# Forgetting attention in a hybrid layer kernel: values with tokens on partitions, the reciprocal sum applied at evacuation, and three PSUM banks in rotation

## The chip, the cores and the metric

The kernel runs on one core of one Trainium2 chip. The metric is the device time of one execution in microseconds. All runs of the kernel before: 3224.91, 3225.07 and 3237.13 us, with the median at 3225.07 us.

## The reference, cut to what matters

The reference advances a two-layer model by one step, for a prompt of 512 tokens and a sample of 32 new tokens behind a cache of 512. Each layer has a mixer (three branches: forgetting attention, differential attention, an RWKV scan), cross attention and a SwiGLU block. The change touches only the forgetting attention ("FoX"), with 8 heads of 64:

```python
def block(qb, dqb, pb):
    s = jnp.einsum('bqhd,bkhd->bhqk', qb, k_all).astype(jnp.float32) * scale
    s = s + jnp.swapaxes(dqb, 1, 2)[:, :, :, None] - d_k[:, :, None, :]
    mask = kpos[None, None, None, :] <= pb[:, None, :, None]
    p = jax.nn.softmax(jnp.where(mask, s, -jnp.inf), axis=-1)
    return jnp.einsum('bhqk,bkhd->bqhd', p.astype(v_all.dtype), v_all)
```

Everything is float32. The output of this branch is later multiplied by a branch weight, with the 512 feature rows on partitions and the T = 544 tokens along the free dimension.

## The kernel before, in words

The kernel is written engine by engine: one instruction stream each for PE (TensorE), ACT (ScalarE), DVE (VectorE), POOL (GpSimd) and SP (DMA issue), each in the order in which its code issues it, tied together by counting semaphores. A loop runs over the two layers. In each layer the forgetting attention runs between the input projections and the differential attention, as four pairs of heads (`it`). Each pair has 10 tiles: for head h, four query tiles of 128 prompt tokens (i = 0..3, with (i+1)·128 keys) and one tile of the 32 sample tokens (i = 4, with 544 keys). `FOX_TILES` (line 104) gives their order.

The work on a pair is a software pipeline over steps k, with the same k in every engine's stream:

- PE, lines 833 to 880: `fox_prologue(h)` at k = 0 and k = 4 transposes values (job "v", line 800), new keys (job "k", line 805) and cached keys (job "p", line 809). At every k: `fox_scores(k)` (lines 823 and 828, with a bf16 mask matmul after it), then `late(s)` (line 774), then `fox_turn(k-2)`, which transposes the exponentials (line 840, or 844 for the sample tile), then `fox_values(k-3)` (line 858, or 862 and 864 for the sample tile). At k = 8, `late` comes ahead of the scores.
- `late(s)` is a quarter of a dense projection of other columns of the input weight: 12 matmuls of four 128-deep slices by three terms of a split float32 product. It accumulates in PSUM bank 7. A half is evacuated by ACT in `late_put` (line 1419) before the next half may begin, and the waits on it (`late_evac`) are in `late`.
- DVE: `fox_scale(h)` (line 1915) at k = 0 and 4; `fox_max(k)` (line 1903), a row maximum; `fox_norm(k-1)` (lines 1910 and 1912), which takes the reciprocal of the sum and multiplies the exponentials by it; `late_split` (line 1891) after k = 3, k = 8 and the last step, which splits the next weight unit of `late` into a high and a low part (lines 1809 and 1819, both of 128x1024); and `fox_evac(h)` (lines 1923 and 1924), once a head, ahead of `fox_max(8)` and at the end. In the first pair of a layer, three memsets of the second buffer (lines 1944 and 1945) stand after the `late_split` of k = 3.
- ACT: `fox_exp(k)` (line 1338) with the sum as accumulator, `late_put` at every second k (even in the first pair, odd in the others), `fox_put(k-2)`, which copies the transposed exponentials out of PSUM, and the copies of the prologue (all line 1341).
- POOL stores, SP loads; each waits on semaphores of the others.

PSUM has 8 banks. Scores use banks 0 to 2 (the sample tile bank 2 and 3), transposes use banks 4 and 5 in turn (`put_bank`), the values of a pair accumulate in bank 6 with head h on partitions 64h to 64h+63 (the sample tile in bank 3), bank 7 is `late`'s.

## Time and profile before

| | |
|---|---|
| median of three runs | 3225.07 us |
| the profiled execution | 3224.55 us |
| its span | 3223.0 us |
| PE busy | 2917.9 us (91%) |
| DVE busy | 1618.5 us (50%) |
| ACT busy | 721.0 us (22%) |
| mean granted clock of PE | 0.96 of full |

A matmul's row shows its latency, and successive matmuls overlap, so the pace of a group is read from the starts of successive rows or from the chain of waits. PE's weight loads have rows of their own (PEld). In forms such as `128*64 128x128`, the first part is the stationary operand (128 rows by 64 columns), the second the moving one. A float32 matmul of the program shows as two matmul rows and two load rows; a transpose shows as one.

### The profile page before, as it was taken

Reading aid. Unit: us, or ns where it says so; the run is one execution under the profiler, and the core shown is the slowest. Engines: PE = TensorE matmul, PEld = TensorE weight load, DVE = VectorE, ACT = ScalarE, POOL = GpSimd, SP = SyncE. Lnnn points to the kernel's source line nnn. Section 1 sums busy time; section 2 is a strip of 40 time slices with the busy share of each in tenths; the row PEclk is TensorE's granted clock in tenths of the full one; section 3 lists DMA queues with packets and bytes.
Section 4 is the critical chain, followed back from the end, with each engine's and each line's share of the span. In section 5 each row is a group of like instructions: output and inputs, shape, how many; then the busy total and the mean of one; then the engine's idle time right before and its main releaser. Section 6 shows DMA issues by size and latency. Waiting matters only on the chain.

```text
span 3223.0 us, 69431 instructions
## 1 busy us (share of the span) xinstructions
PE 2917.9 (91%) x26468; PEld 2692.0 (84%) x26468; DVE 1618.5 (50%) x2997; ACT 721.0 (22%) x1777; POOL 246.4 (8%) x425
## 2 busy tenths in 40 slices
PE   7999998899789889999989999889997898899998
PEld 6877777888788769999978777778897887799998
DVE  4444552666574245553364444426665742455533
ACT  1133332222212230000112333322222122200001
POOL 1121111000000100000001211110000000000000
PEclk9999998999899999999988999999998999899999
DMA  4443326222153213232224333262221521232222
GB/s 122 134 120 91 109 86 148 77 68 64 40 156 95 68 53 92 85 89 79 75 81 122 104 99 111 77 159 74 70 66 47 161 82 53 66 91 85 84 83 64
DMA packets 421640, 292.44 MB, mean 91 GB/s; under 512 B 38640, under 2 KB 386448, under 8 KB 421216
## 3 DMA queue, kind: packets, MB, share of 16 engines
q1 hardware_dynamic: 399072, 229.75, 25.7%
q0 software_dynamic: 22272, 58.70, 5.7%
q8 instruction: 190, 3.11, 0.4%
q14 instruction: 106, 0.87, 0.1%
HBM read 233.23 MB, written 55.18 MB: 89 GB/s over the span
## 4 chain that ended last, share of the span: by engine, by line
PE 74%; DVE 12%; DVEq 4%; issue 4%; ACT 3%; DMA 2%; POOLq 1%; ACTq 1%; SPq 0%; POOL 0%
PE PS L708 32%; PE PS L774 9%; PE PS L1079 7%; PE PS L1020 5%; PE PS L686 4%; DVE WLO L1819 2%; PE PS L1233 2%; ACT U L1338 2%; PE PS L945 1%; PE PS L1058 1%; PE PS L858 1%; PE PS L823 1%; DMA U<-in_rwkv_g_dram 1%; PE PS L1144 1%; ACT U L1341 1%
## 5 line engine op out<-in xcount | busy, mean ns | idle before, releaser
L708 PE MATMUL PS<-U_r,WHI 128*128 128x272 f32 x2656 | 485.3, 294 | 70.4 <-DVEq L1820 35.3
L1809 DVE CAST WHI<-ring 128x1024 fp32r<-128x1024 f32 (+2 forms) x292 | 189.5, 649 | 623.7 <-PE PS L708 472.1
L708 PEld LDWEIGHTS PS<-U_r,WHI 128*128 128x128 f32 x2656 | 395.6, 193 | 78.4 <-issue 50.8
L1341 ACT COPY U<-PS 128x272 f32<-128x272 f32 (+10 forms) x764 | 265.9, 373 | 807.1 <-PE PS L1079 144.9
L708 PE MATMUL PS<-brT_r,WHI 128*128 128x272 f32 x1728 | 360.3, 290 | 1.9 <-ACTq L1720 1.9
L708 PE MATMUL PS<-U_r,WLO 128*128 128x272 f32 x1696 | 356.7, 292 | 0.0
L708 PE MATMUL PS<-hT_r,WHI 128*128 128x272 f32 x1696 | 350.7, 288 | 0.0
L1819 DVE TENSOR_TENSOR WLO<-ring,WHI 128x1024 fp32r<-128x1024 f32 (+2 forms) x292 | 332.3, 1138 | 23.5 <-issue 1.8
L774 PE MATMUL PS<-U_r,WHI 128*128 128x272 f32 x832 | 268.6, 323 | 16.1 <-ACT U L1341 16.1
L708 PE MATMUL PS<-brT_r,WLO 128*128 128x272 f32 x1344 | 278.2, 288 | 0.0
L708 PEld LDWEIGHTS PS<-brT_r,WHI 128*128 128x128 f32 x1728 | 274.7, 190 | 2.3 <-ACTq L1720 2.3
L1020 PE MATMUL PS<-U_r,WHI 128*128 128x272 f32 x768 | 237.4, 309 | 42.2 <-POOLq L401 26.8
L708 PEld LDWEIGHTS PS<-U_r,WLO 128*128 128x128 f32 x1696 | 273.2, 193 | 0.0
L708 PEld LDWEIGHTS PS<-hT_r,WHI 128*128 128x128 f32 x1696 | 267.6, 189 | 0.0
L774 PE MATMUL PS<-U_r,WLO 128*128 128x272 f32 x832 | 247.3, 297 | 0.0
L774 PE MATMUL PS<-hT_r,WHI 128*128 128x272 f32 x832 | 246.5, 296 | 0.0
L1020 PE MATMUL PS<-U_r,WLO 128*128 128x272 f32 x768 | 227.1, 296 | 0.0
L1020 PE MATMUL PS<-hT_r,WHI 128*128 128x272 f32 x768 | 226.2, 295 | 0.0
L1079 PE MATMUL PS<-U 64*64 64x64 f32 (+1 forms) x5184 | 215.9, 238 | 2.4 <-issue 1.8
L1079 PEld LDWEIGHTS PS<-U 64*64 64x64 f32 x5184 | 208.5, 134 | 5.1 <-issue 3.9
L708 PEld LDWEIGHTS PS<-brT_r,WLO 128*128 128x128 f32 x1344 | 209.8, 189 | 0.0
L774 PEld LDWEIGHTS PS<-U_r,WHI 128*128 128x128 f32 x832 | 164.8, 198 | 36.3 <-ACT U L1341 21.9
(321 smaller groups left out, 4407.0 us busy)
## 6 DMA issues: line engine op xcount, KB each, us to landing
ring<-in_w_in_dram SPq DMA_DIRECT2D x126, 512.0 KB, 4.1
ring<-in_w_ffn_in_dram SPq DMA_DIRECT2D x88, 512.0 KB, 3.8
ring<-in_w_ffn_out_dram SPq DMA_DIRECT2D x32, 448.0 KB, 3.6
proj_scratch<-U POOLq DMA_DIRECT2D x104, 136.0 KB, 2.0
U<-proj_scratch SPq DMA_DIRECT2D x48, 272.0 KB, 4.1
gate_scratch<-U POOLq DMA_DIRECT2D x96, 136.0 KB, 3.0
U<-gate_scratch SPq DMA_DIRECT2D x48, 272.0 KB, 2.8
ring<-in_w_branch_dram SPq DMA_DIRECT2D x48, 256.0 KB, 3.0
```

What stands on the lines that cost most here:

```text
L686: ins = mm(PS[0:width, 2 * q + h, 0:HT], ring[:, n % RING, k, 0:width], rhs(k, h), start=(k == 0), stop=(k == kn - 1))
L708: ins = mm(PS[:, 2 * q + h, 0:HT], w, half(x, h), start=(first and k == 0 and n == 0), stop=(last and k == kn - 1 and n == len(terms) - 1))
L774: ins = mm(PS[:, 7, 0:HT], w, half(x, h), start=(k == 0 and i == 0), stop=(k == 7 and i == 2))
L823: mm(PS[:, b, 0:n], q, FK[it % 2][0:66, h, 0:n], start=True, stop=False)
L858: ins = mm(PS[o, 6, i * P:(i + 1) * P], FVT[it % 2][:, h, t, :], FPT[:, k % 2, t * P:(t + 1) * P], start=(t == 0), stop=(t == i))
L1020: ins = mm(PS[:, 6 + h, 0:HT], w, half(x, h), start=(k == 0 and i == 0), stop=(k == 7 and i == 2))
L1079: ins = mm(PS[r, bank, cols], w_c[r], x_c[r], start=(n == 0), stop=(n == len(pairs) - 1))
L1233: ins = mm(PS[:, 2 + n % 4, u * P:(u + 1) * P], MNT[:, k, t * P:(t + 1) * P], ring[:, (U_MEM + 2 * s + u) % RING, k, :], start=(k == 0), s ...
L1338: return act.activation(out, in_, func, **kw)
L1341: return act.copy(out, in_)
L1809: copy(hi, src)
L1819: tt(lo, w, hi.bitcast(F32), ALU.subtract)
```

## The change

- Values: the transposed exponentials become the stationary operand and the values the moving one, so that tokens stand on the partitions of the output (128 tokens by 64 columns) in place of features (64 partitions by 128 columns). Each of the 10 tiles of a pair has its own output, in its own turn of a PSUM bank.
- `fox_norm` goes. `fox_inverse` keeps only the reciprocal. `fox_evac(k)` multiplies by it as it copies the tile's 128x64 result from PSUM into `FO`, 10 times a pair, at DVE step k+4, in place of one copy of 64x512 and one of 64x32 a head.
- `fox_final(pair)` transposes `FO` (five transposes, two bank turns) and ACT copies the result to `brT`. It runs at k = 2 of the next pair, or ahead of the differential attention for the last pair.
- Banks 4, 5 and 6 rotate over all jobs of the layer (`FOX_ORDER`: prologue jobs, transposes t, values o, final jobs f). A job waits for the evacuation of the job three places earlier: by ACT (`fx_put`), or by DVE for an o (`fx_evac`).
- `fox_scores(8)` moves ahead of `late`; `fox_turn` waits for the exponential itself; the sample tile's scores no longer wait for an evacuation of bank 3.
- On DVE the third `late_split` moves from after the last `fox_norm` to step 12, between `fox_evac(8)` and `fox_evac(9)`.

```diff
+def fox_jobs():
+    order = []
+    for it in range(4):
+        for k in range(13):
+            if k in (0, 4):
+                order += [(it, x, k // 4) for x in "vkp"]
+            if k == 2 and it > 0:
+                order += [(it - 1, "f", n) for n in range(2)]
+            if 2 <= k <= 11:
+                order.append((it, "t", k - 2))
+            if k >= 3:
+                order.append((it, "o", k - 3))
+    order += [(3, "f", n) for n in range(2)]
+    return order
+FOX_ORDER = fox_jobs()
+FOX_BANK = {key: 4 + n % 3 for n, key in enumerate(FOX_ORDER)}
+FOX_LAST = {key: FOX_ORDER[n - 3] if n >= 3 else None for n, key in enumerate(FOX_ORDER)}
...
-                    def put_bank():
-                        j = job[0]
-                        job[0] += 1
-                        pe.wait_ge(fx_put, g * 16 + j + 1)
+                    def put_bank(key):
+                        last = FOX_LAST[key]
+                        if last is not None:
+                            if last[1] == "o":
+                                pe.wait_ge(fx_evac, l * FOX_OUTS + FOX_COUNT[last])
+                            else:
+                                pe.wait_ge(fx_put, l * FOX_PUTS + FOX_COUNT[last])
                         settle(pe)
-                        return PS[:, 4 + j % 2, :]
+                        return PS[:, FOX_BANK[key], :]
...
                     def fox_values(k):
                         h, i = FOX_TILES[k]
-                        pe.wait_ge(fx_put, g * 16 + jobs_of[k] + 1 + 2)
-                        if i == 0:
-                            pe.wait_ge(fx_evac, g * 2 + h + 1)
-                        o = slice(64 * h, 64 * h + 64)
+                        pe.wait_ge(fx_put, l * FOX_PUTS + FOX_COUNT[(it, "t", k)])
+                        settle(pe)
+                        b = put_bank((it, "o", k))
                         if i < 4:
                             for t in range(i + 1):
-                                ins = mm(PS[o, 6, i * P:(i + 1) * P], FVT[it % 2][:, h, t, :],
-                                         FPT[:, k % 2, t * P:(t + 1) * P], start=(t == 0), stop=(t == i))
+                                ins = mm(b[:, 0:64], FPT[:, k % 2, t * P:(t + 1) * P], FVT[it % 2][:, h, t, :],
+                                         start=(t == 0), stop=(t == i))
...
+                    def fox_final(pair):
+                        pe.wait_ge(fx_evac, l * FOX_OUTS + 10 * (pair + 1))
+                        settle(pe)
+                        b = put_bank((pair, "f", 0))
+                        for i in range(4):
+                            ins = tr(b[:, i * P:(i + 1) * P], FO[:, i, :], ident)
+                        ins.then_inc(fx_turned, 1)
+                        b = put_bank((pair, "f", 1))
+                        tr(b[:, 0:DEC_SEQ], FO[0:DEC_SEQ, 4, :], ident[0:DEC_SEQ, 0:DEC_SEQ]).then_inc(fx_turned, 1)
...
-                        if k < 10 and k != 8:
+                        if k < 10:
                             fox_scores(k)
                         if k < (12 if it else 11):
                             late(12 * it + k + (0 if it else 1))
-                        if k == 8:
-                            fox_scores(k)
+                        if k == 2 and it > 0:
+                            fox_final(it - 1)
...
-                        ts(FP[0:m, k % 3, 0:n], FP[0:m, k % 3, 0:n], FST[0:m, k % 3, 2:3], None, ALU.mult) \
-                            .then_inc(fx_norm, 1)
...
+                    def fox_evac(k):
+                        h, i = FOX_TILES[k]
+                        m = P if i < 4 else DEC_SEQ
+                        dve.wait_ge(fx_out, g * 10 + k + 1)
+                        ts(FO[0:m, i, 64 * h:64 * h + 64], PS[0:m, FOX_BANK[(it, "o", k)], 0:64], FST[0:m, k % 4, 2:3], None,
+                           ALU.mult).then_inc(fx_evac, 1)
+                    for k in range(14):
                         if k == 0:
                             fox_scale(0)
                         if k == 4:
                             fox_scale(1)
-                        if k == 8:
-                            fox_evac(0)
+                        if k >= 4:
+                            fox_evac(k - 4)
                         if k < 10:
                             fox_max(k)
-                        if k >= 1:
-                            fox_norm(k - 1)
+                        if 1 <= k <= 10:
+                            fox_inverse(k - 1)
+                        if k == 12:
+                            late_split(3 * it + 2)
                         if k in (3, 8):
                             late_split(3 * it + k // 8)
...
-                    late_split(3 * it + 2)
-                    fox_evac(1)
```

## Rows read from the trace of the kernel before

**Rows 1.** The page's chain of work that ended last, shares of the span.
```profile
PE 74%; DVE 12%; DVEq 4%; issue 4%; ACT 3%; DMA 2%; POOLq 1%; ACTq 1%; SPq 0%; POOL 0%
```
**Rows 2.** Windows of the four pairs, layers 0 and 1: start:end, length, busy per engine, clock.
```profile
131.70:305.40 173.70, 163.38 (x1159) 132.31 (x1159) 74.97 (x167) 60.74 (x187) 33.83 (x56) 0.98 0.38 107
1724.80:1901.60 176.80, 166.42 (x1159) 135.11 (x1159) 74.97 (x167) 60.73 (x187) 33.84 (x56) 0.95 0.38 105
```
**Rows 3.** Line 1912, the scaling of the exponentials: instructions, and who waited (none).
```profile
L1912 DVE TENSOR_SCALAR U<-U x80: 285/420/509, 137.0 to 1894.3; 128x128 f32<-128x128 f32 x16, 128x256 f32<-128x256 f32 x16, 32x544 f32<-32x544 f32 x16, 128x384 f32<-128x384 f32 x16
who waited for it (us, times):
```
**Rows 4.** Chain of waits, 300 to 345 us: start, duration, what.
```profile
303.11 0.44 PE PS L840 x4
...
304.36 1.02 PE PS L858 x8
305.37 1.71 PE PS L774 x12
...
326.72 1.08 PE PS L980 x8
...
341.18 1.50 PE PS L774 x12
342.68 0.89 PE PS L976 x8
```
**Rows 5.** Lines 858 and 980, weight loads: ns min/median/max, forms.
```profile
L858 PEld LDWEIGHTS PS<-U x320: 132/137/137, 143.5 to 1901.2; 128*64 128x64 f32 x160
...
L980 PEld LDWEIGHTS PS<-U x64: 186/192/192, 326.7 to 2063.0; 128*128 128x128 f32 x64
```
**Rows 6.** Chain of waits, 200 to 235 us.
```profile
200.19 0.84 PE PS L823 x2
...
210.05 0.70 DVE U L1903
...
213.98 0.39 PE PS L844 x5
...
220.24 0.61 PE PS L809 x4
...
232.59 0.60 PE PS L809 x4
```
**Rows 7.** Timeline of PE, 209.8 to 212.4 us: start, duration, in brackets the idle time before.
```profile
212.20 0.40 PE L774 MATMUL PS<-U_r,WHI 128*128 128x272 f32 x1 [1.25 <-ACT U L1341]
```
**Rows 8.** Timeline of DVE, 215 to 222 and 229 to 238 us.
```profile
217.00 0.69 DVE L1809 CAST WHI<-ring 128x1024 fp32r<-128x1024 f32 x1 [4.66 <-PE PS L774]
217.76 1.22 DVE L1819 TENSOR_TENSOR WLO<-ring,WHI 128x1024 fp32r<-128x1024 f32 x1
219.18 0.69 DVE L1923 COPY brT<-PS 64x512 f32<-64x512 f32 x1 [0.19 <-PE PS L858]
219.79 0.19 DVE L1924 COPY brT<-PS 64x32 f32<-64x32 f32 x1
...
231.71 1.22 DVE L1819 TENSOR_TENSOR WLO<-ring,WHI 128x1024 fp32r<-128x1024 f32 x1
233.05 0.44 DVE L1917 TENSOR_SCALAR U<-U 64x544 f32<-64x544 f32 x1
```
**Rows 9.** Timeline of PE, 214 to 222 us.
```profile
218.04 1.09 PE L858 MATMUL PS<-U 128*64 128x128 f32 x8
...
221.51 0.49 PE L823 MATMUL PS<-U 66*128 66x128 f32 x2 [0.67 <-ACT U L1341]
```
**Rows 10.** Chain of waits, 143 to 152 us (first pair, layer 0).
```profile
146.78 1.82 DVE U L1945
...
151.38 0.65 PE PS L774 x3
```
**Rows 11.** Windows in the first pair of layer 1, columns as rows 2.
```profile
1748.00:1752.00 4.00, 4.00 (x20) 3.17 (x20) 0.64 (x3) 0.74 (x2) 0.00 (x0) 0.50 0.76 172
```

More of the change, by code:

```diff
@@ L255, in build_program @@
         FP, FPT = cv(3, T), cv(2, 5 * P)
-        FST = cv(3, 4)
+        FST = cv(4, 4)
+        FO = cv(5, P)
         ESTL = carver(NU - KM * T - 4 * HT)(4, HT)
@@ L356, in build_program @@
         fx_stored = [sem("fx_stored0"), sem("fx_stored1")]
-        fx_scaled, fx_scores, fx_max, fx_exp, fx_norm, fx_turned, fx_put, fx_out, fx_evac = (
-            sem("fx_" + n) for n in ("scaled", "scores", "max", "exp", "norm", "turned", "put", "out", "evac"))
+        fx_scaled, fx_scores, fx_max, fx_exp, fx_turned, fx_put, fx_out, fx_evac = (
+            sem("fx_" + n) for n in ("scaled", "scores", "max", "exp", "turned", "put", "out", "evac"))
         rope_loaded = sem("rope_loaded")
@@ L1426, in _, with next_job @@
                     g = act.snap(l * 4 + it)
-                    job = [0]
-                    def next_job():
-                        j = job[0]
-                        job[0] += 1
-                        act.wait_ge(fx_turned, g * 16 + j + 1)
-                        return PS[:, 4 + j % 2, :]
+                    def next_job(key):
+                        act.wait_ge(fx_turned, l * FOX_PUTS + FOX_COUNT[key])
+                        return PS[:, FOX_BANK[key], :]
                     def fox_prologue(h):
-                        for to in (FVT, FKT):
-                            b = next_job()
+                        for to, x in ((FVT, "v"), (FKT, "k")):
+                            b = next_job((it, x, h))
                             copy(to[it % 2][:, h, 0:4, :].rearrange("p a b -> p (a b)"), b[:, 0:256])
@@ L1440, in fox_prologue, with fox_final @@
                             act.drain().then_inc(fx_put, 1)
-                        b = next_job()
+                        b = next_job((it, "p", h))
                         copy(FK[it % 2][0:64, h, T:T + PAST], b[0:64, :]).then_inc(fx_put, 1)
+                    def fox_final(pair):
+                        b = next_job((pair, "f", 0))
+                        copy(brT[:, pair, 0:SEQ], b).then_inc(fx_put, 1)
+                        b = next_job((pair, "f", 1))
+                        copy(brT[:, pair, SEQ:T], b[:, 0:DEC_SEQ]).then_inc(fx_put, 1)
                     def fox_exp(k):
@@ L1470, in _ @@
                             late_put(6 * it + k // 2)
+                        if k == 2 and it > 0:
+                            fox_final(it - 1)
                         if k >= 2:
                             fox_put(k - 2)
+                    if it == 3:
+                        fox_final(3)
                 for it in range(DIFF_HEADS // 2):
@@ L1917, in fox_scale @@
                         ts(FQ[it % 2][0:64, h, :], FQ[it % 2][0:64, h, :], HEAD_DIM ** -0.5, None, ALU.mult).then_inc(fx_scaled, 1)
-                    def fox_evac(h):
-                        dve.wait_ge(fx_out, g * 2 + h + 1)
-                        r = slice(64 * h, 64 * h + 64)
-                        copy(brT[r, it, 0:SEQ], PS[r, 6, :])
-                        copy(brT[r, it, SEQ:T], PS[r, 3, 64:96])
-                        dve.drain().then_inc(fx_evac, 1)
-                    for k in range(11):
+                    def fox_evac(k):
[5 more added lines that the diff above has]
+                    for k in range(14):
                         if k == 0:
@@ L2424, in _ @@
                     for h in range(2):
-                        wait(fx_put, g * 16 + (3, 8)[h] + 2)
+                        wait(fx_put, l * FOX_PUTS + FOX_COUNT[(it, "p", h)])
                         for t, op, os_ in ((FVT, p_fox_v, s_fox_v), (FKT, p_fox_k, s_fox_k)):
@@ L2434, in _ @@
                     for h in range(2):
-                        wait(fx_evac, g * 2 + h + 3)
+                        wait(fx_evac, l * FOX_OUTS + 10 * it + 5 * (h + 1))
                         wait(fx_stored[h], (g + 1) * 64)
```

46 lines of the change are left out of this document (21 added, 25 removed).

## The prediction

> **What bounds the kernel now.** I read the page's chain first: 74% of the span is PE's own work [rows 1]. The change lies in the four pairs of the forgetting attention, so next come the windows over them: 173.7 and 176.8 us in the two layers, 350.5 us in all, of which PE is busy 163.38 and 166.42, DVE 74.97 and ACT some 61 us each [rows 2]. So PE bounds this stage, with a loss of about 10 us a layer in gaps. What DVE or ACT save is worth something only where PE stands waiting for them, and what PE gains or loses goes nearly whole to the end, for the next stage follows on the same engine. The steps to price are therefore: work of PE, waits of PE that go, waits of PE that come. The third view is who waited for what the change removes. The scaling by the reciprocal, 80 instructions of 285 to 509 ns, has nobody who waited for it [rows 3]: between the exponential and its transposition PE always has a `late` of 12 matmuls to do. So the headline of the change, a shorter way from exponential to transposition, is worth 0 on the path. It frees DVE only.
>
> **The values on PE, -12.3 us.** The number of matmuls stays. Each had a stationary operand of 64 columns and a moving one of 128; it becomes 128 and 64. The weight load's row gets longer, 137 ns for the form before and 192 for the 128-column form of line 980 [rows 5], but loads overlap: eight of line 980 (128 stationary, 32 moving columns) fill 1.08 us of the chain and eight of line 858 fill 1.02, while eight of line 976, 128 by 128, fill 0.89 [rows 4]. The pace is the same 0.11 us an instruction and the difference is a fixed part. Line 858 is the only one of these that addresses 64 columns of the array; its group costs 0.13 more than the same work on the full array, and the `late` behind it takes 1.71 against 1.50 us behind line 976 [rows 4]. I read both as the price of changing the shape in which the array is addressed, 0.13 on entering and 0.20 on leaving. With tokens on partitions the prompt tiles use the full array. Entering gets cheaper where a full-array transposition stands ahead and nothing holds PE (tiles 3 to 6 of a pair; tiles 1 and 7 follow the sample tile's 32-row transposition, and tiles 0 and 9 run into waits below). Leaving gets cheaper for tiles 1 and 3 to 7; behind 0 and 9 stands a 64-row transposition. So 4 x 0.13 + 6 x 0.20 = 1.7 us a pair, 13.8 for eight pairs, less 0.25 in six pairs, where PE would only come earlier to the wait at step 10: 12.3. Ends: 0, if line 858's extra has another cause, and 10 x 0.33 x 8 = 26, if every tile gains both. The sample tiles change 128 by 64 for 128 by 32 and keep their price.
>
> The Trainium skill ("TensorEngine Tiling (Array Packing)", Key Properties) says that changing the tiling mode drains the engine; by that rule the trace's 0.13 and 0.20 are what it calls a drain, and the saving stands. Another page speaks against the change ("TensorE: Matmul & The Clock Gate", LDWEIGHTS): a load costs by its columns, and overlaps running matmuls only when it goes to another row group. The trace agrees with the first half and not with the second, for line 980's loads of 192 ns follow each other at 0.11 us.
>
> **The wait at step 10, -7.5 us.** In each pair but the first, `late(10)` starts 1.25 us late [rows 7]. Behind it stand ACT's `late_put`, ACT's exponential 9 and DVE's maximum 9, which waits until the `late_split` of step 8 is through, and that began only when the late `scores(8)` had been reduced. With `scores(8)` ahead of `late(8)`, DVE starts its maximum 1.7 us sooner, the split runs beside `late(8)`, and the maximum 9 is up about when the scores 9 are. What is late next is the same chain at 0 to 0.25 us (the 0.25 taken off above). 6 x 1.25 = 7.5; between 4 and 9.
>
> **The final transpositions, +7.0 us.** Four full transpositions, 0.44 us (an estimate: four times the 0.11 us pace of [rows 4]), a bank turn, one of 32 rows (line 844 takes 0.39 for five [rows 6], so 0.08), with its change of shape in and out at 0.13 to 0.20 each: 0.83 a pair, 6.6 for eight. The last one of a layer waits for `fox_evac(9)` behind a split, with one `late` as cover: 0.2 more, 0.4 in all. ACT's copies (about 0.8 a pair) are hidden: ACT is busy 61 of 174 us [rows 2]. Between 5 and 9.
>
> **The wait that comes at step 4, +6.6 us.** The job three places ahead of the second prologue's "p" is o of tile 0, so line 809 of k = 4 now waits for `fox_evac(0)`. On DVE that stands behind the `late_split` of step 3 and `fox_scale(1)`. The split is started by the end of `late(3)` on PE, so it doesn't come sooner with DVE's lighter load; it ends at 231.71 + 1.22 = 232.93, the scaling takes DVE to 233.5 [rows 8], and the evacuation, priced by the copy of 64x32 at 0.19 [rows 8], to 233.7. In the trace line 809 started at 232.59 [rows 6]. PE has nothing else in its stream (scores 4 and `late(4)` are queued behind): +1.1 us in each of six pairs. Ends: 0.5 and 1.5.
>
> **The same between pairs, +4.2 us.** "p" of the next pair's first head waits for `fox_evac(9)`. On DVE the third split now comes after `fox_evac(8)`, which needs the values of tile 8, done when the values of tile 9 begin, 218.04 [rows 9]. Evacuation to 218.4, split 217.00 to 219.18 long, 2.2 us with its drains [rows 8], to 220.6, evacuation to 220.9; before, line 809 started at 220.24 [rows 6]. The scores behind wait for its copy in both, so +0.7 at three places in each layer: 4.2. Between 1 and 6.
>
> **The first pair of a layer, +3.6 us.** There the memsets stand between the split and `fox_evac(0)`. They end at 146.78 + 1.82 = 148.60 [rows 10]. With the scaling of the queries (0.44) and the evacuation (0.2), less one removed multiplication ahead (0.4), "p" can start at 148.9. Then 0.60 (line 809), 0.84 (scores), 1.50 (`late`), 0.39 (line 844), 0.45 (values, half of 0.89), 0.49 (scores) lead to `late(6)` at 153.2 [rows 4, 6, 9], which started at 151.38 [rows 10]: +1.8, twice. Before, a part of that time was lost later, at `late(6)`; now it is lost as one gap of about 4 us. Ends: 1 and 4 each.
>
> **Semaphore instructions on PE, +1.6 us.** Three more ahead of each of 80 values, one more at each transposition. Ahead of line 840 three already stand at no visible gap, for matmuls are queued. 0.02 a tile; from 0 to 0.1 a tile, 8.
>
> **PE's clock, +4 us.** The granted clock in the first pair of layer 1 falls to 0.50, the 1.2 GHz level, after a gap of PE at the memsets [rows 11], and that layer's pairs take 3.1 us more than those of layer 0 [rows 2]. The change makes 14 new gaps of 0.7 to 4 us. I take it that the two long ones and one in three of the rest bring some loss, with 4 us as an estimate from the 3.1 of one such place; ends 0 and 14.
>
> **Sum.** -12.3 - 7.5 + 7.0 + 6.6 + 4.2 + 3.6 + 1.6 + 4 = +7.2 us on the profiled execution: span 3223.0 to 3230.2, with its 1.55 around it 3231.8. The median shown is 0.5 above that execution: 3232 us. That is 0.2% slower, and about 0.5% (16 us) is the least that a measurement of this kernel can tell from no change, so the forecast is "no difference that can be told".
>
> **The rivals.**
> - *The new gaps cool PE.* The mechanism is the wait for `fox_evac(0)` and `fox_evac(9)`, and the price is PE's clock. If all 14 gaps are followed by a stretch at 1.2 GHz at 1.3 us each (a fraction of the 3.1 us), it costs 18 in place of 4, and with the waits at their upper ends (+4): 3250 us. It decides from about ten stretches on. For it: the stage already shows the lower level after gaps. Against: the waits of 1.25 us at step 10 go in exchange. 0.17.
> - *The longer loads count.* If the 128-column loads don't hide where only 64 columns move, 320 loads x 0.055 us [rows 5] = 17.6, so 3250 us. Against it are the eight of line 980 at 1.08 [rows 4]. 0.03.
> - *Changes of shape are worth more and the evacuations are on time.* All ten tiles at 0.33 (-14 against the forecast), no wait at step 4 (-6.6), no loss of clock (-4): 3207 us. It needs DVE to reach `fox_evac(0)` ahead of the split, which its order doesn't allow, so only parts of it can come. 0.09.
> - *The change is not what it says for PSUM:* three banks in place of two give no slack, since each tile now takes two turns in place of one. That is in the forecast; were half of the 0.67 us that the first scores wait today [rows 9] to come once more in every pair and at both prologues, it adds 16 x 0.33 = 5 and gives 3237, inside its range.
>
> **Numbers.** Forecast with its like 0.71, cooling 0.17, loads 0.03, cheaper shapes 0.09. The range: the ends of the single costs, taken together as independent, give -19 and +16: 3213 to 3248. Faster by over 0.5% (below 3209): 0.09. Slower by over 0.5% (above 3241): 0.20. Within: 0.71.
>
> **What would show each step.** Chain or timeline after: (1) values of 128 by 128 stationary in groups of eight at 0.9 to 1.0 us, and the `late` behind them at about 1.5 in place of 1.7; (2) no wait of over 0.3 us at `late(10)`; (3) idle time of PE ahead of line 809's successor of 1.0 to 1.5 us, released by DVE's evacuation, at k = 4 of every pair, near 4 us in the first, and of about 1 us between pairs; (4) final transpositions of 0.8 us a pair; (5) more stretches at the 1.2 GHz level in the windows of the four pairs. The windows should come out 2 to 5 us a layer longer. The prediction is wrong if the gap at k = 4 is missing (DVE then comes sooner than worked out), if `late` behind values stays at 1.7, or if the mean clock of the stage falls by over 0.03.

## The result, and the profile after

The changed kernel takes 3263.72 us (median of 4 runs, 3253.14 to 3275.59) against 3224.99 us for the kernel before on the same chip: a ratio of 1.0118, with a 95% interval of 1.0084 to 1.0152. It is 1.2% slower. The forecast was 3232 us, and 3263.72 lies above its range (3213 to 3248). The profiled execution took 3263.77 us with a span of 3261.8 us, 38.8 us more than before. The mean granted clock of PE over the span fell from 0.960 to 0.946.

Lines of the kernel after stand at other numbers: `late`'s matmuls at 801 (774 before), the transposition "p" at 838 (809), scores at 852 (823), values at 884 (858), the split at 1850 and 1860 (1809, 1819), `fox_scale` at 1955, and the new `fox_evac` at 1962. ACT's copy is 1377 (1341).

The page of the kernel after. The first line gives the shares of the chain of waits [rows 1], the second each engine's busy time:

```profile
PE 73%; DVE 12%; issue 4%; DVEq 4%; ACT 2%; DMA 2%; POOLq 1%; ACTq 0%; SPq 0%; POOL 0%
PE 2947.5 (90%) x26508; PEld 2729.8 (84%) x26508; DVE 1591.5 (49%) x2965; ACT 726.4 (22%) x1793; POOL 246.8 (8%) x425
```

DVE was relieved as the edit says (1618.5 to 1591.5 us), and it brought nothing. PE is busy 29.6 us longer, though the values have the same count of matmuls and the new transpositions are some 6 us (0.76 us a pair). Either its instructions got slower, or its clock did. The windows tell which. From here on "the stage" is the stretch from the first scores of the four pairs to the first matmul of the differential attention's rotation, 175.2 and 178.3 us long in the two layers before, at clocks of 0.98 and 0.95. The same stretches after, and under them two single pairs of layer 0 (columns: stretch and its length; busy us and count of PE, PEld, DVE, ACT and POOL; granted clock; DMA share; GB/s):

```profile
133.00:327.20 194.20, 178.97 (x1190) 151.16 (x1190) 62.87 (x153) 62.86 (x194) 33.79 (x56) 0.87 0.35 96
1747.60:1941.70 194.10, 178.89 (x1190) 151.18 (x1190) 62.86 (x153) 62.83 (x194) 33.83 (x56) 0.87 0.35 96
...
181.67:232.27 50.60, 46.57 (x301) 39.22 (x302) 15.12 (x38) 16.71 (x51) 8.45 (x14) 0.84 0.32 85
282.85:324.86 42.01, 39.93 (x288) 34.23 (x289) 13.57 (x36) 14.72 (x45) 8.45 (x14) 0.96 0.44 129
```

The stage grew by 19.0 and 15.8 us, 34.8 of the 38.8 us, with the clock at 0.87 in both layers. A rough account: at a granted clock c, a stretch of length L loses about (1 − c) · L against full speed. That is 0.02 · 175.2 + 0.05 · 178.3 = 12.4 us before and 0.13 · (194.2 + 194.1) = 50.5 us after. The difference, 38 us (uncertain by some 4 us, since the clocks have two digits, and too high by what idle time does not lengthen), is about the whole loss. Everything else in the change then comes to about nothing, +0.7 us, where the forecast had +3.2 without its clock term. How much too high can be read where the same matmuls ran at another clock: in the second layer PE is busy 178.89 us here and 158.85 in e3 below, 20.0 us less, where the account gives 23.6. Taken down by that share, the clock costs some 32 us and the rest some 6. Without any account, the windows show that of the 34.8 us 9.7 are more idle time of PE (20.7 us before, 30.4 after) and 25.1 more busy time.

The gaps of PE. The last bracket of a row is the idle time ahead of it and what ended it; the first row is the transposition "p" between pairs in the kernel before, the others are of the kernel after:

```profile
220.24 0.60 PE L809 MATMUL PS<-CB,U 128*64 128x128 f32 x4 [0.37 <-ACTq L1440]
...
151.25 1.03 PE L838 MATMUL PS<-CB,U 128*64 128x128 f32 x4 [4.67 <-DVE U L1962]
...
222.47 0.39 PE L801 MATMUL PS<-U_r,WHI 128*128 128x272 f32 x1 [0.18 <-ACT U L1377]
...
231.00 0.60 PE L838 MATMUL PS<-CB,U 128*64 128x128 f32 x4 [0.73 <-DVE U L1962]
...
232.27 0.80 PE L852 MATMUL PS<-U 66*128 66x128 f32 x2 [0.67 <-ACT U L1377]
...
248.10 0.60 PE L838 MATMUL PS<-CB,U 128*64 128x128 f32 x4 [1.55 <-DVE U L1962]
```

These are the waits that were forecast: 4.67 us in the first pair (about 4 forecast), 0.73 us between pairs (with 0.67 more ahead of the first scores, as before), 1.55 us at k = 4. The wait of `late(10)` is down from 1.25 us [rows 7] to 0.18 us, also as forecast. DVE's timeline shows the order behind the gap between pairs:

```profile
228.26 0.27 DVE L1962 TENSOR_SCALAR U<-PS,U 32x64 f32<-32x64 f32 x1 [2.50 <-PE PS L890]
228.47 0.68 DVE L1850 CAST WHI<-ring 128x1024 fp32r<-128x1024 f32 x1
229.22 1.22 DVE L1860 TENSOR_TENSOR WLO<-ring,WHI 128x1024 fp32r<-128x1024 f32 x1
230.57 0.28 DVE L1962 TENSOR_SCALAR U<-PS,U 128x64 f32<-128x64 f32 x1
230.77 0.42 DVE L1955 TENSOR_SCALAR U<-U 64x544 f32<-64x544 f32 x1
```

`fox_evac(8)`, then a split of two long operations, then `fox_evac(9)`, a quarter of a microsecond of work on which the "p" of the next pair waits. The chain of waits through the other place, k = 4, and what comes after it (start, length, engine, what is written, line, count):

```profile
243.62 1.57 PE PS L801 x12
245.19 0.02 issue
245.21 0.69 DVE WHI L1850
...
245.98 1.23 DVE WLO L1860
...
247.33 0.10 DVE U L1955
247.43 0.26 issue
247.69 0.28 DVE U L1962
...
248.10 0.60 PE PS L838 x4
248.70 1.69 PE PS L852 x2
250.39 0.11 PE PS L853
250.50 2.83 PE PS L801 x12
253.32 0.62 PE PS L873 x5
253.94 1.04 PE PS L884 x4
254.98 0.53 PE PS L852 x2
255.51 0.11 PE PS L853
255.62 2.83 PE PS L801 x12
...
260.50 1.57 PE PS L801 x12
```

The reader is to see the line `L801 x12` three times: 1.57 us ahead of the gap, 2.83 us twice behind it, and 1.57 us again later. The same twelve matmuls took 1.8 times as long. PE had stood idle for 1.55 us, and then ran at the lower level, 1.2 GHz, for some 10 us. The gap is 1.55 us long, and each of the two `late` behind it loses 1.26 us more. No row names this as a wait: PE counts as busy.

Read in windows of 1 us, each layer's stage has seven stretches at a granted clock of 0.50. The first, of some 6 us, is the one in which the stage begins, and every kernel of the case has one (3 to 6 us). The six others, of 3 to 10 us each, begin in or just behind a gap: that of the first pair, all three between pairs, and two of the three of 1.54 to 1.55 us at k = 4. Behind the last one, at 297.51 us, the clock stays at 1.00: not every gap is followed by a fall. The kernel before has two such stretches in both layers together. One is that of [rows 11]. The other stands in layer 0, behind 0.36 us of idle time ahead of "p" and 0.67 ahead of the first scores of the second pair:

```profile
177.38 2.57 PE PS L774 x12
```

So the short waits between pairs could bring the clock down before the change too.

### The profile page after: what moved, and what is told of

Its sections match the earlier page's. It is cut to its first block, busy times and chain, and to the rows that moved or that the text cites. A ratio compares the mean times of both kernels' runs of the same rounds, so it can differ in the third digit from the quotient of the medians.

```text
span 3261.8 us, 69793 instructions
## 1 busy us (share of the span) xinstructions
PE 2947.5 (90%) x26508; PEld 2729.8 (84%) x26508; DVE 1591.5 (49%) x2965; ACT 726.4 (22%) x1793; POOL 246.8 (8%) x425
## 4 chain that ended last, share of the span: by engine, by line
PE 73%; DVE 12%; issue 4%; DVEq 4%; ACT 2%; DMA 2%; POOLq 1%; ACTq 0%; SPq 0%; POOL 0%
PE PS L735 31%; PE PS L801 9%; PE PS L1115 6%; PE PS L1056 5%; PE PS L713 4%; DVE WLO L1860 2%; PE PS L1269 2%; ACT U L1374 2%; PE PS L981 1%; PE PS L852 1%; DVE WHI L1850 1%; PE PS L1094 1%; DMA U<-in_rwkv_g_dram 1%; PE PS L1180 1%; PE PS L1211 1%
## 5 line engine op out<-in xcount | busy, mean ns | idle before, releaser
L735 PE MATMUL PS<-U_r,WHI 128*128 128x272 f32 x2656 | 486.0, 294 | 71.4 <-DVEq L1861 36.4
L735 PEld LDWEIGHTS PS<-U_r,WHI 128*128 128x128 f32 x2656 | 396.7, 193 | 79.3 <-issue 51.9
L735 PE MATMUL PS<-hT_r,WHI 128*128 128x272 f32 x1696 | 351.1, 289 | 0.0
L801 PE MATMUL PS<-U_r,WHI 128*128 128x272 f32 x832 | 276.8, 333 | 6.2 <-ACT U L1377 6.2
L1056 PE MATMUL PS<-U_r,WHI 128*128 128x272 f32 x768 | 238.8, 311 | 39.8 <-POOLq L428 27.1
L801 PE MATMUL PS<-hT_r,WHI 128*128 128x272 f32 x832 | 253.9, 305 | 0.0
L801 PE MATMUL PS<-U_r,WLO 128*128 128x272 f32 x832 | 253.8, 305 | 0.0
L1056 PE MATMUL PS<-hT_r,WHI 128*128 128x272 f32 x768 | 227.7, 296 | 0.0
L735 PEld LDWEIGHTS PS<-brT_r,WLO 128*128 128x128 f32 x1344 | 209.8, 189 | 0.0
L801 PEld LDWEIGHTS PS<-U_r,WHI 128*128 128x128 f32 x832 | 173.2, 208 | 25.1 <-issue 11.8
```

What stands on the lines that cost most here:

```text
L735: ins = mm(PS[:, 2 * q + h, 0:HT], w, half(x, h), start=(first and k == 0 and n == 0), stop=(last and k == kn - 1 and n == len(terms) - 1))
L801: ins = mm(PS[:, 7, 0:HT], w, half(x, h), start=(k == 0 and i == 0), stop=(k == 7 and i == 2))
L1056: ins = mm(PS[:, 6 + h, 0:HT], w, half(x, h), start=(k == 0 and i == 0), stop=(k == 7 and i == 2))
```

## The experiments

All ratios are against the kernel before, run beside each kernel. "Loss" is (1 − clock) · length for both layers' stages, as above. The next is the number of stretches at the 1.2 GHz level in both layers, without those in which the stages begin. The last column is PE's idle time ahead of the transposition "p" that DVE ended, in both layers.

| kernel | ratio (95%) | stage, layers 0 and 1, us | clock | loss, us | stretches | idle ahead of "p", us |
|---|---|---|---|---|---|---|
| before | 1 | 175.2, 178.3 | 0.98, 0.95 | 12 | 2 | 0 (5.5 for ACT) |
| after | 1.0118 (1.0084 to 1.0152) | 194.2, 194.1 | 0.87, 0.87 | 50 | 12 | 23.0 in 14 |
| e1_split_k4 | 0.9993 (0.9975 to 1.0012) | 174.4, 171.7 | 0.94, 0.96 | 17 | 5 | 9.1 in 8 |
| e2_split_k11 | 1.0007 (0.9993 to 1.0021) | 179.7, 180.8 | 0.94, 0.94 | 22 | 6 | 18.7 in 8 |
| e3_both | 0.9977 (0.9954 to 0.9999) | 171.8, 166.2 | 0.95, 0.99 | 10 | 1 | 4.8 in 2 |
| b1_wait | 1.0054 (1.0031 to 1.0077) | 190.0, 190.7 | 0.92, 0.92 | 30 | 10 | 20.8 in 12 |
| e4_scores8 | 1.0153 (1.0121 to 1.0185) | 208.5, 198.9 | 0.83, 0.88 | 59 | 15 | 23.1 in 14 |
| e6_memset | 1.0059 (1.0033 to 1.0086) | 184.0, 184.3 | 0.91, 0.91 | 33 | 10 | 15.5 in 14 |
| e5_all | 0.9928 (0.9904 to 0.9952) | 164.8, 165.3 | 0.98, 0.98 | 7 | 1 | 0 |
| e8_p_first | 0.9898 (0.9869 to 0.9927) | 159.9, 159.5 | 0.99, 0.99 | 3 | 0 | 0 |
| b3_p_first | 0.9929 (0.9905 to 0.9953) | 171.1, 170.1 | 0.98, 0.99 | 5 | 0 | 0 |
| e11_scores8 | 0.9950 (0.9931 to 0.9970) | 165.1, 165.2 | 0.99, 0.99 | 3 | 0 | 0 |
| e9_pad | 1.0122 (1.0091 to 1.0153) | 197.5, 197.6 | 0.88, 0.88 | 47 | 14 | 22.9 in 14 |
| e10_evac_first | 1.0066 (1.0039 to 1.0092) | 190.2, 190.4 | 0.88, 0.88 | 46 | 12 | 20.2 in 14 |
| b4_wait_more | 1.0138 (1.0110 to 1.0166) | 196.1, 197.9 | 0.91, 0.90 | 37 | 9 | 29.0 in 14 |
| e12_wait_more | 1.0172 (1.0143 to 1.0202) | 193.8, 201.4 | 0.88, 0.85 | 54 | 13 | 26.5 in 14 |

One thing to keep in mind with the stage columns: they come from one profiled execution of each kernel. Outside the two stages the sixteen profiles take 2861 to 2876 us, in no order with the edits. So the timed ratio says how much a kernel gained, within its interval, and the stages say where; the two differ by 10 to 15 us in some comparisons, and no run shows why.

### Taking the two waits away: e1, e2 and both

The theory: DVE's order makes PE wait at k = 4 and between pairs, and these gaps bring the clock down. The split of k = 3 is put behind `fox_evac(0)` by a later step, the third split ahead of `fox_evac(8)`; no work is added or dropped.

```diff
# e1_split_k4
-                        if k in (3, 8):
+                        if k in (4, 8):
# e2_split_k11
-                        if k == 12:
+                        if k == 11:
                             late_split(3 * it + 2)
# e3_both: the two together
```

> The changed kernel with DVE's first late_split of a pair moved from after step 3 to the end of step 4, behind fox_evac(0) and the maximum 4; nothing else. Theory A (the changed kernel's 39 us come from the clock: the two prologue transpositions p wait on DVE for an evacuation behind a split, and after each such gap PE goes to 1.2 GHz): the wait at k = 4 goes in all pairs but stays in the first, whose memsets remain ahead of fox_evac(0). Of the four stretches at the lower level behind step 4 in each layer, two (pairs 2 and 3, some 10 us long each, costing 5 us each) go, and 1 us of gap in each of six pairs: about 25 us less than the changed kernel, 3239 us. Theory B (PE goes slower because of its new mix of work, 64 moving columns and more transpositions, and the gaps are a consequence): at most the 6 to 7 us of the gaps go, 3257 us or more, and the stretches at 1.2 GHz stay.

> The changed kernel with DVE's third late_split of a pair moved from step 12 to step 11, ahead of fox_evac(8); nothing else. Theory A: the wait for fox_evac(9) between pairs goes (0.5 to 0.9 us at three places a layer); the stretches at 1.2 GHz of 3.4 to 6.8 us behind those places shrink or go (about 2.5 us each): 12 to 18 us less than the changed kernel, about 3249 us. The wait for ACT's copy (0.67 us) stays, so some of the stretches may stay. Theory B: 3 to 4 us less, about 3260.

> Both moves of late_split together. Theory A: the mean granted clock of the stage returns to about 0.97 and what is left is the predicted PE work: 12 us of saved changes of shape and the wait at step 10 against 7 us of final transpositions and the first pair's gap of 4 us a layer: 3220 to 3232 us. Theory B: 3250 us or more, with the clock of the stage still below 0.92.

Measured: each alone brings the kernel back to the time of before (3220.29 us with e1, 3228.15 with e2, against 3223.71), both together to 3216.98. The stage of layer 0 in e1, in e2, and of layers 0 and 1 in e3:

```profile
132.30:306.70 174.40, 166.09 (x1190) 140.53 (x1190) 63.29 (x153) 62.74 (x194) 34.42 (x56) 0.94 0.39 107
```

```profile
131.60:311.30 179.70, 165.52 (x1190) 140.55 (x1190) 63.10 (x153) 62.70 (x194) 33.75 (x56) 0.94 0.39 105
```

```profile
131.50:303.30 171.80, 164.56 (x1191) 139.84 (x1191) 63.49 (x153) 62.79 (x194) 34.41 (x56) 0.95 0.40 110
1721.20:1887.40 166.20, 158.85 (x1190) 134.99 (x1190) 63.44 (x153) 62.63 (x194) 34.10 (x56) 0.99 0.41 114
```

The same 1190 matmuls keep PE busy 178.97 us after and 158.85 us in layer 1 of e3, a stage that differs in the place of the splits alone. So the work itself was never slower. The order of the splits costs 1.0118 − 0.9977 = 0.0141 of the time, 46 us (50.3 by the stages), where the idle time ahead of "p" falls by 23.0 − 4.8 = 18.2 us. The gaps cost 2.5 times their own length. All three kernels are faster than was expected of them (3239, 3249 and 3220 to 3232 us), so these expectations priced the gaps too low as well.

The two do not add. Over e3, the gaps at k = 4 alone (e2) cost 0.0030, those between pairs alone (e1) 0.0016, the two together 0.0141. The rest, 0.0095 or 31 us, is there only when both kinds of gap are (by the stages 22.5, 8.1 and 50.3 us, so 20 us). The clock shows the same. In e2 the six gaps of 1.55 us at k = 4 behind the first pair are all still there, and not one is followed by a fall. First such a gap and the window around it in e2, then the window at the same place of the kernel after:

```profile
237.40 0.60 PE L838 MATMUL PS<-CB,U 128*64 128x128 f32 x4 [1.55 <-DVE U L1962]
...
236.00:246.00 10.00, 8.60 (x67) 7.35 (x68) 3.31 (x11) 3.69 (x12) 3.22 (x6) 1.00 0.40 109
```

```profile
248.00:258.00 10.00, 9.90 (x42) 8.30 (x43) 1.41 (x5) 2.15 (x7) 2.57 (x4) 0.53 0.32 80
```

The same gap costs its own length in one kernel and several times that in the other, by what stands around it. Between pairs e2 and e3 are not free of idle time: PE waits there 1.06 us for ACT's copy, in place of 0.73 and 0.67.

### The wait alone, in the old work: b1

```diff
                         b = put_bank()
+                        pe.wait_ge(fx_scaled, g * 2 + h + 1)
+                        settle(pe)
                         for t in range(4):
                             ins = tr(b[0:64, t * P:(t + 1) * P], FPK[it % 2][:, h, t, :], ident)
```

The kernel before, with its "p" made to wait for `fox_scale(h)`, which stands behind the same splits. Nothing else of the change is in it.

> The kernel before, with one added wait: the prologue's transposition p of either head waits until DVE has scaled that head's queries, which stands behind the same late_split (and, in the first pair, the memsets). Nothing else is changed: values, banks and final copies are those of before. The added gaps are 0.5 us between pairs, 1.0 us at k = 4 and 4 us in the first pair, in all 15 to 20 us of PE time if they only add up, part of it given back at late(6) of the first pair. Theory A: PE's clock falls behind the gaps here too, and the kernel gets 25 to 40 us slower, 3250 to 3265 us, with half-rate stretches at the same places as in the changed kernel. Theory B: the clock stays, and the time is 3225 plus 9 to 14 us, 3234 to 3239.

Measured: 3244.32 us, 1.0054. PE's gaps in it, and its stage of layer 0:

```profile
183.86 0.60 PE L811 MATMUL PS<-CB,U 128*64 128x128 f32 x4 [0.79 <-DVE U L1919]
...
197.24 0.60 PE L811 MATMUL PS<-CB,U 128*64 128x128 f32 x4 [1.35 <-DVE U L1919]
```

```profile
132.30:322.30 190.00, 172.56 (x1170) 140.24 (x1171) 75.67 (x169) 60.77 (x187) 33.73 (x56) 0.92 0.36 98
```

PE is busy 172.56 us on unchanged work (the four pairs took 163.38 in a window 1.5 us shorter before [rows 2]), and the clock fell from 0.98 to 0.92. The waits alone do this; the new shapes, banks and evacuations are not needed. The size lies between the two expectations (25 to 40 us slower with the clock, 9 to 14 without). The gaps are nearly the same: 1.35 us at k = 4 in place of 1.55, 0.8 between pairs, 4.64 in the first pair. They cost 0.0054 or 17 us, where the change costs 38; by the stages, 27.2 us where the change costs 34.8.

### The rest of the change: e4, e6, e5, e8 and b3

```diff
# e4_scores8: scores(8) goes back behind late(8)
-                        if k < 10:
+                        if k < 10 and k != 8:
                             fox_scores(k)
...
+                        if k == 8:
+                            fox_scores(k)
# e6_memset: the memsets of the first pair at step 0
-                        if (it, k) == (0, 3):
+                        if (it, k) == (0, 0):
# e5_all: e3 and e6
# e8_p_first: e5, and the prologue's jobs in another order, in every engine's stream
-                order += [(it, x, k // 4) for x in "vkp"]
+                order += [(it, x, k // 4) for x in "pvk"]
```

> The changed kernel with scores(8) back behind late(8); both moved splits as in the changed kernel. Step pricing (the wait at step 10 is worth 1.25 us in each of six pairs, the rest stays): 6 to 8 us more than the changed kernel, 3270 us. A rival for the size of the clock's loss (gaps repeat at a distance at which each falls into a bad moment of the clock's control, and another length of a pair breaks that): fewer stretches at 1.2 GHz although the work got more, 3240 to 3255 us.

> The changed kernel with the three memsets of the first pair moved from step 3 to step 0, into idle time of DVE; both splits as in the changed kernel. Adding up: the first pair's gap of 4.7 us falls to 1.2 us and its stretch at 1.2 GHz shrinks, 3.5 to 6 us in each layer: 3252 to 3257 us. If the loss hangs on the distances between gaps, the later pairs may change too, in either direction.

> The kernel with both splits moved (3217 us) and the memsets moved to step 0 as well. The last gap ahead of the transposition p (2.4 us in each layer) goes and with it the stretches at 1.2 GHz behind it (10 us in layer 0): 3205 to 3211 us. If the clock were not behind it, only the 5 us of the gaps: 3212.

> As e5_all, and the prologue's order p, v, k in place of v, k, p, so that ACT has copied the cached keys before the first scores are due. The wait of 0.67 us (with PE's load 0.9) ahead of the first scores goes in eight pairs, and ACT's copies of v and k are hidden behind the scores: 5 to 8 us less than e5_all, 3198 to 3205 us. If PE's own work sets that place, nothing.

With `scores(8)` late again the kernel is slower still, 3284.37 us, though its interval overlaps that of the change; the stages are 19.1 us longer. That part of the change was a gain, which e11 below settles. Moving the memsets takes 3.7 us a layer of idle time away and gains 0.0059 of the time, 19 us, again 2.5 times the idle time (20.0 us by the stages). With all gaps ahead of "p" gone the kernel is at 0.9928, and with "p" first in the prologue at 0.9898, 3199.77 us. Below are the stage of layer 0 in e8, and its chain over a change of pairs:

```profile
129.50:289.40 159.90, 158.11 (x1193) 134.52 (x1191) 63.28 (x153) 63.03 (x198) 34.10 (x56) 0.99 0.44 120
```

```profile
206.26 1.08 PE PS L884 x8
207.34 0.44 PE PS L828 x4
207.77 0.44 PE PS L833 x5
208.22 0.30 PE PS L838 x5
208.52 0.42 PE PS L852 x2
```

Values, "p" (line 828 here), the other two transpositions and the scores follow each other without a gap. "p" leads, so ACT copies it while PE transposes the rest, and the 0.67 us ahead of the first scores are gone. PE is busy 158.11 of 159.90 us. This is the fastest kernel of the case: 1.0% faster than the one before, 2.2% faster than the change.

Of that 1.0%, how much is the change's own? b3 gives the kernel before the two edits that do not need the change, the memsets at step 0 and "p" first.

```diff
-                            pe.wait_ge(fx_put, g * 16 + (3, 8)[h] + 2)
+                            pe.wait_ge(fx_put, g * 16 + (1, 6)[h] + 2)
...
-                        if (it, k) == (0, 3):
+                        if (it, k) == (0, 0):
# and fox_prologue transposes and copies p, v, k in place of v, k, p
```

> The kernel before (values with features on partitions, two banks, scaling of the exponentials) with the same two repairs as e8_p_first: the memsets at step 0 and the prologue's order p, v, k. Against e8_p_first it shows what the change's own parts are worth when no gap is added. By my terms, the values (-12.3), the wait at step 10 (-7.5) and the final transpositions (+7.0) make 13 us, and this kernel should stand at e8's ratio plus 0.004: 0.994 (3212 us against 3225). If the change's savings are an illusion it comes out like e8: 0.990.

It measured 0.9929, 3201.53 us. The change with its gaps mended is better by 0.0031, about 10 us, with intervals that overlap (0.9869 to 0.9927 against 0.9905 to 0.9953). In the stage the difference is 11.2 and 10.6 us a layer, more than the whole program shows; of these 21.8 us, 5.9 are given back outside the stages in the two profiles. The stages divide into 12.6 us less busy time and 9.2 less idle time.

### e11: the moved scores, without gaps around them

```diff
# e8 with scores(8) behind late(8)
-                        if k < 10:
+                        if k < 10 and k != 8:
                             fox_scores(k)
...
+                        if k == 8:
+                            fox_scores(k)
```

> The kernel without the new gaps (splits and memsets moved, p first; ratio 0.9898) with scores(8) back behind late(8): prices that part of the change away from the clock's losses. My price: 1.25 us in each of six pairs, 7.5 us, ratio 0.992. If it is worth more through the clock, ratio 0.994 or above; if late(10) finds another wait, nothing, 0.990.

It measured 0.9950 against 0.9898: 0.0052, 17 us, of which 10.9 us stand in the two stages at an unchanged clock of 0.99. In layer 0 the waits of `late` for ACT are 5.9 us in four places (the longest 1.7 us), against 1.5 us in four in e8. By time the move of `scores(8)` is worth more than all by which e8 is ahead of b3; by the stages it is half of it, 10.9 of 21.8 us. It is not free of the change's other parts: step 8 is the sample tile of the second head, whose scores in the kernel before use bank 3 and wait there for `fox_evac(0)`, which the change does away with. What the move alone would bring in the kernel before was not tried.

### How the length of a gap counts: e9, e10, b4, e12

Three questions were open. Is it the mere length of the work between gaps, is it the length of the gap, and why did b1 lose less?

```diff
# e9_pad: 12 transpositions in place of 1 for tile 5 of each pair, of the same data
-                            for t in range(i + 1):
+                            for t in (range(i + 1) if k != 5 else [0] * 12):
# e10_evac_first: fox_evac(k - 4) ahead of fox_scale(1) at k = 4
# b4_wait_more (on b1) and e12_wait_more (on the change), in fox_scale
+                        for _ in range(2):
+                            copy(small[:, 40:41], small[:, 24:25])
+                            dve.drain()
```

> The changed kernel with more work: the one transposition of tile 5 of each pair is issued 12 times in place of once, at a place of the pair where PE doesn't wait (11 x 0.11 = 1.2 us a pair, 9.7 us in all). All gaps and waits stay. If the loss at the clock has a fixed size per gap, the time rises by 10 us, to about 3273 (ratio to before 1.015). If it hangs on the distance from gap to gap (a longer pair puts the gaps elsewhere against the clock's own steps), the time in the stage at 1.2 GHz changes by more than 10 us a layer, in either direction, and the kernel may even get faster: ratio below 1.008 or above 1.022.

> The changed kernel with fox_evac(0) ahead of fox_scale(1) at DVE's step 4, both still behind the split. The gap at k = 4 shrinks from 1.54 to about 1.15 us in each pair, nothing else changes: by adding up 0.4 x 8 = 3 us, ratio 1.011. If the gap's size decides whether the clock falls, well over 10 us less (ratio below 1.009).

> As b1_wait (the kernel before, with p waiting for DVE's scaling), and two small copies of one column, each with its drain, ahead of each scaling, so that both gaps grow by some 0.4 to 0.6 us: to about 1.3 us between pairs and 1.9 us at k = 4. Theory 1, the size of the gap decides whether PE's clock falls, whatever work PE has: the time rises by far more than the 6 us of added gap, to a ratio of 1.013 or above. Theory 2, the new form of the values or the new order is what makes the clock fall there: gaps cost their own length in the kernel before, 1.0054 becomes 1.007 to 1.009.

> The changed kernel with the same two small copies ahead of each scaling: the gap at k = 4 grows from 1.54 to about 2.0 us. Theory 1: the clock falls already at nearly every gap, so what is left to lose is the added gap, 4 us, and some longer stretches: ratio 1.013 to 1.019. If the loss depended on a narrow coincidence, moving the gaps' lengths by half a us either way would relieve it (e10_evac_first moved it down by 0.4 us and gained 0.005): ratio below 1.010.

e9 lengthened the stage by 3.4 us a layer and changed nothing beyond that: 1.0122, loss 47 us. At this one length, the distance from gap to gap did not matter for the whole. e10 shortened each gap at k = 4 from 1.55 to 1.20 us (4.67 to 4.33 in the first pair). That is 8 · 0.35 = 2.8 us of idle time. Against the change its ratio is lower by 0.0052, 17 us, with intervals that overlap a little (up to 1.0092, from 1.0084), and its stages are 7.7 us shorter. Against e9, run beside it, the time fell by 16 us, from 3263.4 to 3247.4, and the stages by 14.5, but 6.8 of these are e9's added work. So e10 gained more than its idle time, between 8 and 17 us. e12 lengthened the same gaps to 2.00 us and the time rose to 1.0172, with an interval (1.0143 to 1.0202) that just meets the change's. b4 lengthened the gaps of b1 by 0.45 us, those at k = 4 and those between pairs alike. This one is the clearest, for nothing of the change is in it: 8 us of idle time more by the table (6.4 by the total of what DVE and ACT ended, 30.2 against 23.8), and 0.0084 or 27 us lost, from 1.0054 to 1.0138, with intervals far apart. Its stages are 13.3 us longer. First b4, then e12, then e10:

```profile
182.65 0.60 PE L811 MATMUL PS<-CB,U 128*64 128x128 f32 x4 [1.26 <-DVE U L1922]
...
198.07 1.00 PE L811 MATMUL PS<-CB,U 128*64 128x128 f32 x4 [1.81 <-DVE U L1922]
```

```profile
247.06 0.60 PE L838 MATMUL PS<-CB,U 128*64 128x128 f32 x4 [2.00 <-DVE U L1965]
```

```profile
246.38 0.60 PE L838 MATMUL PS<-CB,U 128*64 128x128 f32 x4 [1.20 <-DVE U L1962]
```

Put in order of the gap at k = 4, six kernels with all the gaps (e4, e6 left out) are in the order of their times too, but for the first two, which are level:

| gap at k = 4, us | kernel | ratio | both stages, us |
|---|---|---|---|
| 1.20 | e10 (on the change) | 1.0066 | 380.6 |
| 1.35 | b1 (on before) | 1.0054 | 380.7 |
| 1.55 | after, e9 | 1.0118, 1.0122 | 388.3, 395.1 |
| 1.81 | b4 (on before) | 1.0138 | 394.0 |
| 2.00 | e12 (on the change) | 1.0172 | 395.2 |

By time the step from 1.35 to 1.55 us looks steep: 0.0064 or 21 us. The stages show 7.6 us between the same two kernels, and the rest of the 21 lies outside them. By the stages no step is steep, and the loss for each microsecond of idle time ahead of "p" lies between 1.5 and 2.8 us: 2.8 for e3, 2.7 for e6 and e10, each against the change; 2.1 for b4 against b1; 2.0 for e12 against the change; 1.6 for e2 against e3; 1.5 for b1 against the kernel before. So a longer gap costs more, and more than its own length. Part of it is the clock: the loss column has 37 us for b4 and 30 for b1, 46 for e10 and 50 for the change.

What stays open is what decides whether a given gap is followed by a fall. Gaps of 1.54 us are followed by one at two places of three in a layer of the change and at none in e2. The places of the falls differ from kernel to kernel, and each length was tried at one or two points only. The table mixes old and new work, and the gaps between pairs are not the same in all of it (0.73 in the change, 0.8 in b1, 1.3 in b4). The difference between e12 and the change lies within their intervals.

## Why the prediction was wrong

The step that failed is **"PE's clock, +4 us"**. It measured about +38 us by the (1 − c) · L account, and some 32 by the busy time of the same matmuls. All others together, forecast at +3.2 us, came to +0.7 by the one and some +6 by the other, so the failed term makes up the miss of 32 us (3263.7 against 3231.8), or by the second account all but some 3 us of it.

- *The values, -12.3.* Right in mechanism. A group of eight takes 0.84 us in place of 1.02, and the `late` behind it 1.56 in place of 1.71 [rows 4]: 0.33 together, as forecast. As a total it may be low: PE is busy 12.6 us less in the stages of e8 than in those of b3, though e8 has the 6 us of final transpositions, and 1 to 2 us of the 12.6 are clock. That makes about 17 us by estimate. Rows of the change's chain in layer 0:

```profile
163.45 0.62 PE PS L884 x6
...
214.94 0.84 PE PS L884 x8
...
225.44 1.56 PE PS L801 x12
```

- *The wait at step 10, -7.5.* Right: 0.18 us are left of 1.25. e11 shows that the move of the scores behind it is worth more, 10.9 us in the stages.
- *The final transpositions, +7.0.* Right: 0.44 and 0.17 us in the chain, and some 0.15 of a change of shape, 0.76 a pair against 0.83. ACT's copies were hidden.
- *The wait at step 4, +6.6.* Right in place, cause and size: a gap of 1.55 us where 0.34 stood on average before (5.5 us in 16), +1.2 against +1.1. The evacuation itself took 0.28 us, not 0.19.
- *Between pairs, +4.2.* Right in cause: 0.73 us of idle time, where 0.37 stood before the row at 220.24 [rows 6]. That is half of the 0.7 forecast. The other 0.67 us, ahead of the first scores, stayed.
- *The first pair, +3.6.* The gap is 4.67 us, forecast about 4. What it cost without the clock was not separated.
- *Semaphores, +1.6.* No gap shows at the values in the chain; too small to be told apart.
- *PE's clock.* I read the one stretch at the lower level in layer 1 [rows 11], took its price, and let a third of the short gaps have some of it. Three things were wrong. The count: 12 of the 14 gaps are followed by such a stretch, not six. The price: a stretch behind a short gap is not cheaper than one behind a long gap. The two `late` behind that at 248.10 lose 2 · 1.26 = 2.5 us, the scores between them more, and the 12 stretches cost 3 to 4 us each, where the term had 4 us for all. And the gaps are not single cases to be counted: e1, e2 and e3 show that 31 of 46 us (by the stages 20 of 50) come only when both kinds are there. The trace of before had a sign that I passed over, a `late` of 2.57 us at 177.38 behind 0.36 and 0.67 us of idle time. The rival "the new gaps cool PE" had the mechanism. Its price of 1.3 us a place, 18 us for 14 places, was half of what came, and its chance of 0.17 was too low for a stage in which 14 new gaps of PE were forecast.

The forecast's own tests were good: it named a fall of the stage's clock by over 0.03 as what would prove it wrong, and the clock fell by 0.11 and 0.08. Its range was added up wrongly: the ends of the eight terms, taken as independent, give −15 and +18, so 3217 to 3250 us and not 3213 to 3248. The result lies above both.

The Trainium skill ("TensorE: Matmul & The Clock Gate", A second HAM failure mode: psum-queue depth-cycling) describes a case of this kind, in a bf16 kernel: a kernel that cycles through PSUM banks leaves PE idle for very short times between groups of matmuls, often enough that the clock goes back and forth between its levels, and the loss is in throughput between bursts. The change's chain agrees with it (1.57, 2.83, 2.83, 1.57 us for one `late`); b1 adds that the waits are enough, without a change of banks. The prediction weighed this page for the weight loads alone, and not for this.

## What to carry to other kernels

When a change puts a short operation that PE waits for behind a long one on another engine, price the gap at more than its length, since PE's clock can fall after it: here 2.5 times by time for the gaps taken away whole (e3, e6), and 1.5 to 2.8 times by the length of the stages, for changes of length too. Do not take it as a rule for a single gap: in e2 gaps of 1.55 us were followed by no fall. Look for the order on the waiting side first. Two splits moved by one step on DVE were worth 46 us, more than any other term of the forecast. And read the granted clock by stage before counting instructions: the same `late` group at two lengths in one chain is the sign.

## What the runs showed of the hardware

- The clock fell to the 1.2 GHz level in a stage in which PE was busy 92% of the time, behind gaps of 1.5 us and behind pairs of gaps of 0.7 and 0.67. The group of twelve then took 2.83 us in place of 1.57. Not every gap was followed by a fall: 12 of 14 in the change, none of six at k = 4 in e2.
- Gaps do not add. Those at k = 4 alone cost 10 us over e3, those between pairs alone 5 us, both 46 us (by the stages 22, 8 and 50).
- Without the gaps (e8) the stage ran at 0.99 and PE was busy 99% of it, at 158.11 us for the matmuls that took 178.97 in the change.
- A 128x64 evacuation with a multiplication from PSUM takes 0.28 us on DVE, and a 32x64 one 0.27, with a quarter of the partitions.
